# Delta rule levels on blocks of 64x64, two over each other

## The reference

```python
A = jnp.where(strict, jnp.einsum('bhnid,bhnjd->bhnij', k_beta, kc) * L, 0.0)
rhs = jnp.concatenate([vc * bc[..., None], k_beta * jnp.exp(G)[..., None]], axis=-1)
sol = lax.linalg.triangular_solve(eye + A, rhs, left_side=True, lower=True, unit_diagonal=True)
u, w = sol[..., :dv], sol[..., dv:]
attn = jnp.where(causal, jnp.einsum('bhnid,bhnjd->bhnij', qc, kc) * L, 0.0)
def step(S, inp):                       # over the chunks, S is 128x128 a head
    v_new = u_n - jnp.einsum('bhcd,bhdv->bhcv', w_n, S)
    o = jnp.einsum('bhcd,bhdv->bhcv', q_n, S) + jnp.einsum('bhij,bhjv->bhiv', a_n, v_new)
    S = S * d_n[..., None, None] + jnp.einsum('bhcd,bhcv->bhdv', k_n, v_new)
```

## Time and profile before

| | |
|---|---|
| median of 3 runs | 2320.45 us (2319.55 to 2320.57) |
| the profiled execution | 2317.8 us, its span 2316.0 us, mean granted clock 0.994 |
| PE busy | 2270.0 us, 98% of the span, 10550 matmul records |
| DVE busy | 966.2 us, 42% |
| ACT busy | 860.3 us, 37% |
| POOL busy | 993.3 us, 43% |

### The profile page before, as it was taken

One profiled execution on the slowest core, in us unless ns is written; L12 is line 12 of the kernel. 1 busy time (PEld: TensorE's weight loads), 2 busy tenths in 40 slices (PEclk: granted clock), 3 DMA queues, 4 the chain that ended last, 5 costly groups with the idle time before them and its releaser, 6 DMA issues.

```text
span 2316.0 us, 24835 instructions
## 1 busy us (share of the span) xinstructions
PE 2270.0 (98%) x10550; PEld 1870.5 (81%) x10550; DVE 966.2 (42%) x1165; ACT 860.3 (37%) x1042; POOL 993.3 (43%) x416
## 2 busy tenths in 40 slices
PE   9999999999999999999999999998998999999997
PEld 7888778888888887888888757877878888888886
DVE  4241323441143203443234632288488233766601
ACT  4354333323322433432245364353361434322221
POOL 5437234544444651444433613444133334454542
PEclk9999999999999999999999999999999999999999
DMA  6215123322232431323233302342231233333231
GB/s 226 99 64 166 62 76 97 98 93 100 92 100 98 144 117 42 97 95 100 93 112 127 91 28 82 108 125 58 65 113 35 64 126 101 95 97 100 92 99 73
DMA packets 159998, 222.96 MB, mean 96 GB/s; under 512 B 24065, under 2 KB 85633, under 8 KB 159633
## 3 DMA queue, kind: packets, MB, share of 16 engines
q1 hardware_dynamic: 158336, 216.63, 29.4%
q10 hardware_dynamic: 1552, 4.76, 0.6%
HBM read 214.50 MB, written 6.85 MB: 96 GB/s over the span
## 4 chain that ended last, share of the span: by engine, by line
PE 86%; DVE 9%; ACT 3%; DMA 1%; issue 1%; POOL 0%; ACTq 0%; DVEq 0%
PE ps L1086 72%; PE ps L1280 2%; PE ps L1283 2%; DVE VB L2067 1%; PE ps L1296 1%; PE ps L1319 1%; DVE QN L2067 1%; PE ps L1469 1%; PE ps L1391 1%; PE ps L1404 1%; DVE KN L2067 1%; PE ps L1595 0%; DMA at_dram<-AT 0%; DVE MT L2175 0%; DVE QN L2064 0%
## 5 line engine op out<-in xcount | busy, mean ns | idle before, releaser
L559 POOL TENSOR_TENSOR w_lo<-w_raw,w_hi 128x1024 fp32r<-128x1024 f32 x378 | 951.5, 2526 | 1271.5 <-ACT w_hi L628 1271.2
L628 ACT ACTIVATE w_hi<-w_raw 128x1024 fp32r<-128x1024 f32 x378 | 395.9, 1056 | 887.9 <-DMA w_raw<-w_in 127.6
L1086 PE MATMUL ps<-XH,w_hi 128*128 128x512 f32 x1784 | 700.3, 393 | 1.5 <-ACT RLN L882 0.9
L1086 PE MATMUL ps<-XH,w_lo 128*128 128x512 f32 x1784 | 694.3, 389 | 0.0
L1086 PE MATMUL ps<-XL,w_hi 128*128 128x512 f32 x1784 | 694.0, 389 | 0.0
L1086 PE MATMUL ps<-HID,w_hi 128*128 128x512 f32 x1728 | 533.0, 390 | 0.1
L1086 PEld LDWEIGHTS ps<-XH,w_hi 128*128 128x128 f32 x1784 | 334.9, 188 | 74.3 <-issue 2.9
L1086 PEld LDWEIGHTS ps<-XL,w_hi 128*128 128x128 f32 x1784 | 335.0, 188 | 71.4 <-issue 2.9
L1086 PEld LDWEIGHTS ps<-XH,w_lo 128*128 128x128 f32 x1784 | 334.9, 188 | 70.0
L1086 PEld LDWEIGHTS ps<-HID,w_hi 128*128 128x128 f32 x1728 | 324.2, 188 | 68.4 <-issue 1.0
L1086 PE MATMUL ps<-HID,w_lo 128*128 128x512 f32 x864 | 336.2, 389 | 0.0
(11 more groups left out here) (357 smaller groups left out, 2262.9 us busy)
## 6 DMA issues: line engine op xcount, KB each, us to landing
w_raw<-w_in SPq DMA_DIRECT2D x72, 512.0 KB, 3.6
w_raw<-ffn_w_up SPq DMA_DIRECT2D x128, 256.0 KB, 2.8
w_raw<-w_up SPq DMA_DIRECT2D x88, 256.0 KB, 3.0
w_raw<-xa_wkv SPq DMA_DIRECT2D x32, 512.0 KB, 3.6
w_raw<-ffn_w_down SPq DMA_DIRECT2D x32, 512.0 KB, 3.9
w_raw<-w_in_c SPq DMA_DIRECT2D x24, 512.0 KB, 3.8
w_raw<-w_down SPq DMA_DIRECT2D x22, 512.0 KB, 3.8
w_raw<-xa_wq SPq DMA_DIRECT2D x16, 512.0 KB, 3.9
```

Of the source, the lines that this page charges most:

```text
L559: nc.gpsimd.tensor_tensor(w_lo[:, s, :, :], w_raw[:, s, :, :], w_hi[:, s, :, :].bitcast(F32), ALU.subtract).then_inc(lo_done, 1)
L628: nc.scalar.activation(w_hi[:, s, :, :], w_raw[:, s, :, :], ACT.Copy).then_inc(hi_done, 1)
L1086: mm = nc.tensor.matmul(ps[:, bank + m, :], a, b, start=start and j == 0 and n == 0, stop=stop and j == 1 and n == 2)
```

## The change

All products and matrices of the levels before the last have blocks of 64x64. A 128x128 matrix of a chunk then has two blocks that matter, its upper left and its lower right one; these are laid over each other, the first in partitions 0 to 63 and the second in 64 to 127, in 64 columns. MM, T1 and the new MTP (in place of MT in the first two levels) hold 4 x 64 columns a head in place of 4 x 128. `LEVELS` loses its third entry, and the masks and BD are cut to 64 columns.

- `level_inner` and `level_outer` do two products where one stood, on partitions 0 to 63 and 64 to 127, each 64x64 by 64 columns. The plain product of level 1 is formed for the first half only.
- All levels use bank set A: inner results in columns 0 to 255 of a bank, outer results in columns 256 to 511. So they need ATT to have been read from A, not the gate from B.
- The last level is one product of 64x64 a chunk in each step (`last_inner`, `last_outer`): VectorE copies the inner result into T1, and ScalarE writes the negative of the outer result into the upper right quarter of MT. VectorE writes the diagonal quarters of MT in level 1; the lower left ones are set to zero once, at the start of q = 0.
- On TensorE the values are transposed between the inner and the outer step of level 1, into bank set B. On VectorE two taps of the values stand ahead of the block inverses, the normalising of the queries right behind them, ATT after tap 8, and `scaled` behind the first masking.

```diff
-LEVELS = (16, 32, 64)
+LEVELS = (16, 32)
...
-        MM = at("MM", 48, [P, 4, T])
-        T1 = at("T1", 56, [P, 4, T])
+        MM = at("MM", 48, [P, 4, NCH * HALF])
+        MTP = at("MTP", 52, [P, 4, NCH * HALF])
+        T1 = at("T1", 56, [P, 4, NCH * HALF])
...
                 # GpSimd, expand: m is MM, then MTP
-                            pk[:, 4 * hh:4 * hh + 4, :].unsqueeze(2).broadcast_to([P, NCH, P // FIRST, FIRST]),
-                            BD[:, :, :].unsqueeze(1).broadcast_to([P, NCH, P // FIRST, FIRST]), ALU.mult).then_inc(mx_pool, 1)
+                            pk[:, 4 * hh:4 * hh + 4, :].unsqueeze(2).broadcast_to([P, NCH, HALF // FIRST, FIRST]),
+                            BD[:, :, :].unsqueeze(1).broadcast_to([P, NCH, HALF // FIRST, FIRST]), ALU.mult).then_inc(mx_pool, 1)
...
                 # ScalarE
-                scaled_rows(VB, 0, 16 * q + 12)
+                scaled_rows(VB, 0, 16 * q + 12, B)
+                for hh in range(4):
+                    act.wait_ge(lv_pe, 24 * q + 20 + hh + 1)
+                    nc.scalar.activation(tri(MT, hh)[0:HALF, :, HALF:P], packed(ps[:, A + hh, 256:512])[0:HALF, :, :],
+                                         ACT.Copy, scale=-1.0).then_inc(rows_act, 1)
...
                 # TensorE
-                def level_inner(hh, bank):
+                def level_inner(hh):
                     for n in range(NCH):
-                        mm = nc.tensor.matmul(ps[:, bank + hh, in_chunks(n)], AT[:, hh, in_chunks(n)], MM[:, hh, in_chunks(n)],
-                                              start=True, stop=True)
+                        for half in (lower, upper):
+                            mm = nc.tensor.matmul(ps[half, A + hh, columns(n, half)], AT[half, hh, diagonal(n, half)],
+                                                  MM[half, hh, columns(n, half)], start=True, stop=True)
                     mm.then_inc(lv_pe, 1)
...
-                pe.wait_ge(at_dve, 8 * q + 8)
-                pe.wait_ge(dq_act, 3 * q + 3)
-                transposed(VB)
-
-                pe.wait_ge(ga_dve, q + 1)
                 nl = 32 * q
                 for hh in range(4):
+                    pe.wait_ge(at_dve, 8 * q + 4 + hh + 1)
                     pe.wait_ge(mx_pool, 8 * q + hh + 1)
-                    level_inner(hh, B)
+                    level_inner(hh)
...
                 for hh in range(4):
                     pe.wait_ge(lv_dve, nl + 4 + 2 * hh + 2)
-                    level_inner(hh, B)
+                    level_inner(hh)
+                pe.wait_ge(ga_dve, q + 1)
+                pe.wait_ge(dq_act, 3 * q + 3)
+                transposed(VB, B)
                 for hh in range(4):
                     pe.wait_ge(lv_dve, nl + 12 + hh + 1)
-                    level_outer(hh, A, B)
+                    level_outer(hh, plain=True)
                 for hh in range(4):
-                    pe.wait_ge(lv_dve, nl + 16 + 2 * hh + 2)
-                    level_inner(hh, A)
+                    pe.wait_ge(lv_dve, nl + 16 + 3 * hh + 3)
+                    last_inner(hh)
                 for hh in range(4):
-                    pe.wait_ge(lv_dve, nl + 24 + hh + 1)
-                    level_outer(hh, B)
+                    pe.wait_ge(lv_dve, nl + 28 + hh + 1)
+                    last_outer(hh)
...
                 # VectorE
                 evacuate(2)
+                taps(2, 0, 2)
                 block_inverses()
-                taps(2, 0, 8)
                 normalise(1, QN, LNq, float(P) ** -0.5)
-                taps(2, 8, 16)
+                taps(2, 2, 8)
                 for hh in range(4):
                     dve.wait_ge(kv_pe, 16 * q + 8 + hh + 1)
                     nc.vector.tensor_tensor(ATT[:, hh, :], ps[:, A + hh, :], DL[:, hh, :], ALU.mult).then_inc(at_dve, 1)
+                taps(2, 8, 16)
...
-                scaled(SGD[:, 4 * q:4 * q + 4, :], B, ga_dve)
...
                 for hh in range(4):
-                    lower_block(0, hh, B)
+                    lower_block(0, hh)
+                scaled(SGD[:, 4 * q:4 * q + 4, :], B, ga_dve)
                 for hh in range(4):
-                    take_off(0, hh, A)
+                    dve.wait_ge(lv_pe, npe + 4 + hh + 1)
+                    nc.vector.tensor_tensor(MTP[:, hh, :], MTP[:, hh, :], ps[:, A + hh, 256:512], ALU.subtract).then_inc(lv_dve, 1)
                     dve.wait_ge(lv_dve, nl + 4 + 2 * hh + 1)
-                    nc.vector.transpose(MM[:, hh, :], MT[:, hh, :]).then_inc(lv_dve, 1)
+                    nc.vector.transpose(MM[:, hh, :], MTP[:, hh, :]).then_inc(lv_dve, 1)
...
                 for hh in range(4):
-                    take_off(1, hh, A)
-                    nc.vector.tensor_tensor(MM[:, hh, :], MM[:, hh, :], ps[:, B + hh, :], ALU.subtract).then_inc(lv_dve, 1)
+                    dve.wait_ge(lv_pe, npe + 12 + hh + 1)
+                    for half in (low, high):
+                        nc.vector.tensor_tensor(tri(MT, hh)[half, :, half], packed(MTP[:, hh, :])[half, :, :],
+                                                packed(ps[:, A + hh, 256:512])[half, :, :], ALU.subtract).then_inc(lv_dve, 1)
+                    nc.vector.tensor_tensor(MM[low, hh, :], MM[low, hh, :], ps[low, A + hh, 0:256], ALU.subtract).then_inc(lv_dve, 1)
                 for hh in range(4):
-                    lower_block(2, hh, A)
+                    dve.wait_ge(lv_pe, npe + 16 + hh + 1)
+                    nc.vector.tensor_copy(T1[high, hh, :], ps[high, A + hh, 0:256]).then_inc(lv_dve, 1)
                 late(2)
                 late(3)
-                for hh in range(4):
-                    take_off(2, hh, B)
```

More of the change, by code:

```diff
@@ L86 @@
 FIRST = 16
-LEVELS = (16, 32, 64)
+LEVELS = (16, 32)
+HALF = P // 2
 AT_PLANE = P * P + P
@@ L253, in program @@
         PKM, PKT = at("PKM", 64, [P, 4 * NCH, FIRST]), at("PKT", 65, [P, 4 * NCH, FIRST])
[L254 to L255 removed]
+        LVM = at("LVM", 66, [P, len(LEVELS), HALF])
+        BD = at("BD", 67.5, [P, HALF // FIRST, FIRST])
         FSA = at("FSA", 69.5, [P, FIRST, FIRST])
@@ L438, in gain_of, with packed, tri @@
             return sm[:, 100 + c:101 + c] if name is None else pcol(name, c)
+        def packed(ap):
+            return ap.rearrange("p (n c) -> p n c", n=NCH)
+        def tri(x, hh):
+            return x[:, hh, :].rearrange("p (n c) -> p n c", n=NCH)
         def delta_banks(q):
@@ L602, in expand @@
             def expand(q):
-                for i, (pk, m) in enumerate(((PKM, MM), (PKT, MT))):
+                for i, (pk, m) in enumerate(((PKM, MM), (PKT, MTP))):
                     pool.wait_ge(pk_loaded, 32 * (q + 1))
@@ L948, in inverse_norm, with scaled_rows @@
                         nc.scalar.activation(ln[:, part, :], ln[:, part, :], ACT.Exp, scale=-0.5).then_inc(l2_r, 1)
-                def scaled_rows(dst, a, ready):
+                def scaled_rows(dst, a, ready, bank):
                     for hh in range(4):
@@ L953, in scaled_rows @@
                         for c in range(NCH):
-                            last = nc.scalar.activation(dst[:, hh, c * P:(c + 1) * P], ps[:, A + hh, c * P:(c + 1) * P],
+                            last = nc.scalar.activation(dst[:, hh, c * P:(c + 1) * P], ps[:, bank + hh, c * P:(c + 1) * P],
                                                         ACT.Copy, scale=TC[:, a, c, 4 * q + hh:4 * q + hh + 1])
@@ L1446, in keys_by_keys, with transposed @@
                         mm.then_inc(kv_pe, 1)
-                def transposed(x):
+                def transposed(x, bank):
                     for hh in range(4):
                         for n in range(NCH):
-                            mm = nc.tensor.transpose(ps[:, A + hh, in_chunks(n)], x[:, hh, in_chunks(n)], ident)
+                            mm = nc.tensor.transpose(ps[:, bank + hh, in_chunks(n)], x[:, hh, in_chunks(n)], ident)
                         mm.then_inc(kv_pe, 1)
@@ L1465, in keys_by_queries, with columns, diagonal @@
                         mm.then_inc(kv_pe, 1)
-                def level_inner(hh, bank):
+                lower, upper = slice(0, HALF), slice(HALF, P)
+                def columns(n, half, base=0):
+                    return slice(base + n * HALF, base + n * HALF + HALF)
+                def diagonal(n, half):
+                    return slice(n * P + half.start, n * P + half.stop)
+                def level_inner(hh):
                     for n in range(NCH):
-                        mm = nc.tensor.matmul(ps[:, bank + hh, in_chunks(n)], AT[:, hh, in_chunks(n)], MM[:, hh, in_chunks(n)],
-                                              start=True, stop=True)
+                        for half in (lower, upper):
+                            mm = nc.tensor.matmul(ps[half, A + hh, columns(n, half)], AT[half, hh, diagonal(n, half)],
+                                                  MM[half, hh, columns(n, half)], start=True, stop=True)
@@ L1471, in level_inner, with level_outer @@
```

(20 more changed lines are left out.)

23 lines of the change are left out of this document (10 added, 13 removed).

## The result

The changed kernel takes 2291.92 us (median of 4 runs, 2289.85 to 2292.94); the kernel before took 2320.0 us beside it. The ratio is 0.9881, 95% interval 0.9869 to 0.9893: 28 us less, where 29.5 us and 2290.9 us were forecast. Its profiled execution took 2292.94 us for a span of 2291.0, at a mean granted clock of 0.994. PE was busy 2251.2 us (10806 records), DVE 948.1, ACT 863.5, POOL 989.3.

The account below looks back on a forecast made before the run. TensorE bounds the kernel (86% of the span), waiting on VectorE in the delta stage. Gains of 14.1 us (q = 0) and 15.4 us (q = 1) sum to 29.5: 2320.45 - 29.5 = 2290.9 us; case range 2288.6 to 2294.0, overall 2282 to 2304.

Parts of the forecast that it names:

- the gains of both passes: Delta stage, scan start earlier by 14.1 us in q = 0 and 15.4 us in q = 1.
- The price of a small record: TensorE's level products: 352 records a pass at 0.062 us each, 21.8 us in place of 25.0.
- pairs overlap: Rival, level products: halves run together at 0.034 us a record, VectorE sets everything; 36.8 us gain, 2283.6 us; chance 0.26.
- The bound: Levels: TensorE sets the pace; behind level 1's outer products VectorE needs 1.0 us a head, TensorE 1.49.
- The taps: VectorE's last eight value taps ahead of the levels: 5.4 us plus 3.2 us of GpSimd collisions, ending at 1594.8 in q = 0.
- The gain of part 1: VectorE's new order before the levels: last gate unit ends 2.8 us earlier in q = 0, 4.1 us in q = 1.
- the clock should stay up: TensorE at VB's transposes within the levels: granted clock does not fall, since no idle stretch is over 1 us.
- both gains should reach the end: Behind the scan's start: nothing else changes and TensorE has no wait, so the whole 29.5 us reaches the kernel's end.

## Why the prediction was right, and where its steps were not

The number held, 2290.9 for 2291.92, and so did the gains of both passes, within 0.2 us. The mechanism did not: TensorE was to set the pace of the levels, and VectorE does. Steps that were mis-sized in opposite directions cancelled, so that the number held is luck.

- *The price of a small record.* The step said 0.062 us for each of 352. It is 0.029 us where both halves alternate (256 of them) and 0.058 to 0.060 us on one half alone (96). The case "pairs overlap" had this right (0.034), and the row that it was held against, the 8x8 transposes at 0.0675 us, is no floor for the issue of a record; inside their run they start 0.062 us apart. The Trainium skill, TensorE: Matmul & The Clock Gate, Part 3 ("The mechanism"), agrees with the trace: products on other tiles run together, and the two of a pair start 0.007 us apart. The Trainium skill, TensorEngine Tiling (Array Packing), "Gotcha 1: PSUM Pressure", says that different row tiles cannot use one bank at a time; both halves here write the same bank, other partitions of it, at 0.029 us a record, so the measurement decides against it for this case. The two halves differ in rows, in columns and in the partitions that they write; row tiles that write the same partitions were not run.
- *The bound.* With products this cheap, VectorE had to be it. The prediction gave that case 16.3 us from the end of the taps to the scan; the trace shows 18.7 (1597.44 to 1616.10). A head costs 1.23 us behind the outer step, not 1.02, and 0.81 in level 0, not 0.7: an operation of 256 elements takes 0.33 to 0.45 us, not 0.34 throughout.
- *The taps.* 8.6 us forecast, 9.9 and 8.6 found. In q = 0 the expansions began at 1585.6, not 1582.3, so they met more taps. Turns with GpSimd were the right cause: beside an expansion a tap takes 1.15 us, alone 0.66, and holding back one split of 2.8 us took 2.1 us from the run of taps.
- *The gain of part 1.* It was counted as 2.8 and 4.1 us of waiting and clock. The two runs on VectorE's order show that it is none: with the old order the changed kernel takes 73.5 us for the four stretches, with the new one 76.0. The wait only moves to the next place where TensorE needs VectorE.
- *The clock.* That "the clock should stay up" was wrong; it fell in both passes, in the levels and again at the start of the scan. In the levels VectorE's own work covers most of it, at the scan nothing does.
- *The way to the end.* That "both gains should reach the end" did not hold: the first stretch of the scan has the same products, but at the fallen clock it took 2.1 and 1.1 us more than before. With products on one half alone the fallen clock cost 12 us of the sum of the stretches, more than the dearer products themselves.
- *What brought the gain,* then, as the timelines have it (no run takes these apart): VectorE's operations of the levels with half the elements, expansions with half the elements, and the inner step of level 0 and VB's transposes in time that TensorE waited or VectorE needed anyway.

The profiled execution after was 1.5 us late at the start of the retention (first record at 1343.4, 1341.9 before), in code that is the same; the stretches above are free of it, and its cause is open. The other profiled executions begin it anywhere from 1341.7 to 1344.1.

## What to carry to other kernels

When an edit makes the busiest engine's work cheaper, work out the chain through the other engine first: here twice the price of a product added 15 us of products and 3 us of time, and an operation of 2.3 us on VectorE moved the scan in full. A wait that goes is a gain only if the next thing its engine needs is there earlier too. Products on one half of the array ran at half the rate here without a partner on the other half. And look behind the stretch that an edit shortens: a clock that falls in its new waits is paid for in code that the edit leaves alone.

## What the hardware showed that was not expected

- Single-half products of 64x64, back to back for 13.7 us, did not bring the granted clock from 0.5 to 1.0; with the clock at 1.0 at their start, it stayed there through the levels. With both halves alternating it was back after 3.0 us of products (q = 0 of the change).
- Halves issued four records apart ran at 0.039 us a record, between 0.029 (alternating) and 0.059 (one half).
- A tap on VectorE that meets a weight split on GpSimd takes 2.8 us in place of 0.7 (2.82 us from 1593.87 in q = 0 of the change), and the split itself 2.8 us in place of 2.4. Such a meeting costs the run of taps 2.1 us.
- 64x64 products that alternate between the two diagonal quarters of the array write one PSUM bank, other partitions of it, at 0.029 us a record.
